# VectorE's order at the stage borders: norm-weight products and low parts of the second token tile taken by halves around the last weight split

## The reference

```
for each of the four layers:
    h = rms_norm(x, w_mix)             # x * rsqrt(mean(x^2) + eps) * w
    x = x + mixer(h)                   # gated delta rule; latent attention; differential
                                       # attention; sliding-window attention with sinks
    x = x + (silu(g) * u) @ w_down     # g, u = halves of rms_norm(x, w_ffn) @ w_gate_up
between the two blocks:  x = rms_norm(x, final_norm)
```

## Time and profile before

| | us |
|---|---|
| median of 3 runs (lowest to highest) | 1441.63 (1440.91 to 1443.24) |
| the profiled execution, its own time | 1442.56 |
| its span, first to last instruction | 1440.8 |
| TensorE busy | 1410.2 |
| VectorE busy | 927.9 |
| ScalarE busy | 728.2 |

### The profile page before, as it was taken

One profiled execution on the slowest core, in us unless ns is written; L12 is line 12 of the kernel. 1 busy time (PEld: TensorE's weight loads), 2 busy tenths in 40 slices (PEclk: granted clock), 3 DMA queues, 4 the chain that ended last, 5 costly groups with the idle time before them and its releaser, 6 DMA issues.

```text
span 1440.8 us, 19866 instructions
## 1 busy us (share of the span) xinstructions
PE 1410.2 (98%) x7787; PEld 1202.1 (83%) x7787; DVE 927.9 (64%) x1630; ACT 728.2 (51%) x1246; POOL 22.9 (2%) x44
## 2 busy tenths in 40 slices
PE   8899999999999999999999999899999999999999
PEld 8899999888888888888888878688888877888887
DVE  7767777756755547666555499775555587665553
ACT  7564646434544436545444465745444456454442
POOL 3200000000000000000000000000000000000000
PEclk9999999999999999999999999999999997999999
DMA  8433323225665554436665445246655541465552
GB/s 236 125 103 88 88 87 91 74 74 161 190 188 182 185 176 153 155 102 198 184 189 190 161 162 181 68 125 205 187 186 188 167 140 51 126 204 178 188 190 88
DMA packets 168838, 216.61 MB, mean 150 GB/s; under 512 B 11219, under 2 KB 136746, under 8 KB 168746
## 3 DMA queue, kind: packets, MB, share of 16 engines
q1 hardware_dynamic: 166976, 213.03, 47.7%
q10 hardware_dynamic: 1770, 2.32, 0.6%
HBM read 214.26 MB, written 1.05 MB: 149 GB/s over the span
## 4 chain that ended last, share of the span: by engine, by line
PE 83%; DVE 11%; DMA 2%; ACT 2%; issue 1%; POOL 1%; SPq 0%; ACTq 0%; DVEq 0%
PE psum L898 22%; PE psum L900 22%; PE psum L899 22%; PE psum L1112 4%; DVE w_low L646 4%; PE psum L1104 2%; PE psum L1296 2%; PE psum L1272 2%; PE psum L1118 1%; PE psum L1233 1%; DVE hT L2110 1%; PE psum L1285 1%; DVE work L818 1%; PE psum L1086 1%; DVE x L2088 1%
## 5 line engine op out<-in xcount | busy, mean ns | idle before, releaser
L646 DVE TENSOR_TENSOR w_low<-ring,w_high 128x1024 fp32r<-128x1024 f32 (+3 forms) x395 | 475.0, 1212 | 320.3 <-ACT w_high L632 318.2
L632 ACT ACTIVATE w_high<-ring 128x1024 fp32r<-128x1024 f32 (+3 forms) x395 | 411.1, 1048 | 441.1 <-PE psum L900 430.7
L898 PE MATMUL psum<-w_high,hT 128*128 128x512 f32 (+2 forms) x944 | 372.3, 394 | 1.5 <-DVE hT L2110 1.0
L900 PE MATMUL psum<-w_high,hT 128*128 128x512 f32 (+2 forms) x944 | 366.1, 388 | 0.0
L899 PE MATMUL psum<-w_low,hT 128*128 128x512 f32 (+2 forms) x944 | 365.5, 387 | 0.0
L898 PEld LDWEIGHTS psum<-w_high,hT 128*128 128x128 f32 x944 | 177.3, 188 | 37.3 <-DVE hT L2110 3.8
L898 PE MATMUL psum<-w_high,parts 128*128 128x512 f32 (+1 forms) x532 | 208.1, 391 | 0.3 <-DVE work L2673 0.3
L900 PEld LDWEIGHTS psum<-w_high,hT 128*128 128x128 f32 x944 | 177.2, 188 | 36.6
L900 PE MATMUL psum<-w_high,parts 128*128 128x512 f32 (+1 forms) x532 | 206.0, 387 | 0.0
L899 PE MATMUL psum<-w_low,parts 128*128 128x512 f32 (+1 forms) x532 | 205.8, 387 | 0.0
L899 PEld LDWEIGHTS psum<-w_low,hT 128*128 128x128 f32 x944 | 177.5, 188 | 33.8
(11 more groups left out here) (278 smaller groups left out, 1418.2 us busy)
## 6 DMA issues: line engine op xcount, KB each, us to landing
ring<-in_ffn_w_gate_up SPq DMA_DIRECT2D x176, 256.0 KB, 3.2
ring<-in_w_gate_up SPq DMA_DIRECT2D x176, 256.0 KB, 3.2
ring<-in_gdn_w_in SPq DMA_DIRECT2D x48, 512.0 KB, 3.9
ring<-in_ffn_w_down SPq DMA_DIRECT2D x44, 512.0 KB, 3.3
ring<-in_w_down SPq DMA_DIRECT2D x44, 512.0 KB, 3.3
ring<-in_da_w_qkv SPq DMA_DIRECT2D x24, 512.0 KB, 4.1
ring<-in_gdn_w_out SPq DMA_DIRECT2D x16, 512.0 KB, 3.3
ring<-in_mla_w_out SPq DMA_DIRECT2D x8, 512.0 KB, 4.3
```

The lines of the kernel that those rows point to most:

```text
L632: nc.scalar.activation(piece_slot(w_high, n), piece_slot(ring, n), ACT.Copy).then_inc(s.w_hi, 1)
L646: nc.vector.tensor_tensor(piece_slot(w_low, n), piece_slot(ring, n), piece_slot(w_high, n).bitcast(F32), ALU.subtract).then_inc(s.w_lo, 1)
L898: mm(out, lhs[0], rhs[0], start=start, stop=False)
L900: return mm(out, lhs[1], rhs[0], start=False, stop=stop)
```

## The change

For the six GAINED borders VectorE's order for tile 1 changes from "split, product 0, product 1, low 0, low 1" to "product 0, split, low 0, product 1, low 1". `turned_low` is cut into `gained` and `low_half`, which hold the same two instructions. At k = 5 `final_gains(0)` moves from behind turned_low of tile 0 to behind tile 1's last low part, right in front of `final_gains(1)`; ScalarE's square of the first tile's product moves with it, behind the square of x of tile 1. It gets a wait of ScalarE on itself between the two squares of the products, as both write the same scratch tile `junk_y`. k = 7 keeps its order.

```diff
--- before.py
+++ after.py
@@ -1586,9 +1586,14 @@
                 if t and k not in GAINED:
                     act.wait_ge(s.ssq_done, 2 * TURN[k] + 1)
                 last = f(junk, x[:, t, :], ACT.Square, accum_out=ssq[:, t:t + 1])
-                if k == 5:
-                    act.wait_ge(s.y_ready, t + 1)
-                    last = f(junk_y, xy[:, t, :], ACT.Square, accum_out=ssq_y[:, t:t + 1])
+                if k == 5 and t:
+                    for n in range(T):
+                        act.wait_ge(s.y_ready, n + 1)
+                        if n:
+                            own.wait()
+                        last = f(junk_y, xy[:, n, :], ACT.Square, accum_out=ssq_y[:, n:n + 1])
+                        if n == 0:
+                            own(last)
                 last.then_inc(s.ssq_done, 1)
 
             def scaled_in(k):
@@ -2099,16 +2104,23 @@
 
             def turned_low(k, t):
 
-                at = 4 * TURN[k] + 2 * t
                 for h in range(2):
                     if k in GAINED:
-                        dve.wait_ge(s.xT_psum, at + h + 1)
-                        tt(quads(xg[:, t, h, :]), quads(B[4 + 2 * t + h][:, :]), gain_row(k, h), ALU.mult).then_inc(s.xg_ready, 1)
+                        gained(k, t, h)
                 for h in range(2):
-                    dve.wait_ge(s.h_hi, at + h + 1)
-                    turned_x = xg[:, t, h, :] if k in GAINED else B[4 + 2 * t + h][:, :]
-                    tt(turned_tiles(hT, 1, t, h), quads(turned_x), turned_tiles(hT, 0, t, h).bitcast(F32),
-                       ALU.subtract).then_inc(s.h_lo, 1)
+                    low_half(k, t, h)
+
+            def gained(k, t, h):
+
+                dve.wait_ge(s.xT_psum, 4 * TURN[k] + 2 * t + h + 1)
+                tt(quads(xg[:, t, h, :]), quads(B[4 + 2 * t + h][:, :]), gain_row(k, h), ALU.mult).then_inc(s.xg_ready, 1)
+
+            def low_half(k, t, h):
+
+                dve.wait_ge(s.h_hi, 4 * TURN[k] + 2 * t + h + 1)
+                turned_x = xg[:, t, h, :] if k in GAINED else B[4 + 2 * t + h][:, :]
+                tt(turned_tiles(hT, 1, t, h), quads(turned_x), turned_tiles(hT, 0, t, h).bitcast(F32),
+                   ALU.subtract).then_inc(s.h_lo, 1)
 
             def root_of(y, w):
 
@@ -2163,15 +2175,21 @@
                     return
                 residual(pr, 0, s.x_ready)
                 turned_low(k, 0)
-                if k == 5:
-                    final_gains(0)
                 split_low(dve, end - 4 + SPLIT)
                 split_low(dve, end - 3 + SPLIT)
                 residual(pr, 1, s.x_ready)
                 split_low(dve, end - 2 + SPLIT)
-                split_low(dve, end - 1 + SPLIT)
-                turned_low(k, 1)
+                if k in GAINED:
+                    gained(k, 1, 0)
+                    split_low(dve, end - 1 + SPLIT)
+                    low_half(k, 1, 0)
+                    gained(k, 1, 1)
+                    low_half(k, 1, 1)
+                else:
+                    split_low(dve, end - 1 + SPLIT)
+                    turned_low(k, 1)
                 if k == 5:
+                    final_gains(0)
                     final_gains(1)
                 inverse_roots(k)
```

## The result

| | before | after |
|---|---|---|
| median of 11 runs, us (lowest to highest) | 1442.84 (1440.91 to 1444.12) | 1444.93 (1443.49 to 1447.14) |
| ratio after to before, 95% interval | | 1.0021 (1.0012 to 1.0029) |
| the profiled execution, us (span) | 1442.56 (1440.8) | 1444.89 (1443.1) |

The change makes the kernel slower by 0.21%; a second round of runs of the same kernel gave 1.0028 (1.0017 to 1.0040). Forecast were 1445.3 us and +3.63.

A forecast was written before the change was run, and what follows sets the result against it. TensorE was taken to set the time, except at stage borders where it waits for VectorE. Feed-forward borders 2.40 + k = 2 0.60 + k = 5 0.63 = 3.63 us on the median 1441.63 gave 1445.3; range 1442.9 to 1447.6.

The forecast's parts named there:

- What bounds the kernel: TensorE sets the time except at stage borders, where it waits for VectorE's second low half and pays any lateness in full.
- The common part, 0.60 per border: Six borders: last low part 0.60 us later each (0.45 to 0.75); 2.40 over the feed-forward borders k = 1, 3, 6, 8.
- s + 3.71: Forecast start of the last low part, from start s of the old order's last split; s + 3.12 in the old order.
- bare copy: ScalarE's copy of half 1 with nothing beside it on VectorE, between product 1 and low 1; 0.69 from product to low part.
- k = 2, 0.60: Behind k = 2 roots, split and the 6.15 us weight transfer all hang on the late square: 0.60 us again.
- The first rival: Partly absorbed: lateness behind k = 2 and k = 5 disappears in stretches waiting for transfers; 1444.0 us, chance 0.13.
- k = 5, 0.63: At k = 5 the roots start 0.63 us later, from the uncovered copy and ScalarE's hand-over to itself; range 0.5 to 1.0.
- The clock: Claim that k = 2's longer stall lowers TensorE's clock to 1.2 GHz for 10.2 us; 1447.3 us, chance 0.05.
- The second rival: The longer stall at k = 2 lowers TensorE's clock; 1447.3 us, chance 0.05.
- The faster rival: Handover pipelined by halves: new order only closes holes, 6 x 0.10, plus 0.5 at k = 5; 1440.5 us, chance 0.05.
- The profiled execution: Whole kernel: the profiled execution of 1442.56 us becomes 1446.2, by the summed 3.63.

The follow-up runs named there:

- Run 3: Against the changed kernel: new order kept at the six borders, final norm's products and squares left where they were before; 1.0029 (1.0019 to 1.0039) of before.
- run 7: Against the kernel before: last split moved behind the low parts, at k = 5 behind the second final product too; 0.9979 (0.9969 to 0.9988), 1437.96 us against 1441.06.
- Run 5: Against run 3's kernel: still by halves, but a split between each product and its low part; 1.0003 (0.9994 to 1.0011) of before.
- run 4: Against the changed kernel: old order at the borders, only the final norm's products and squares moved; 0.9998 (0.9989 to 1.0007) of before.
- run 6: Against run 3's kernel: both products, then the last split, then both low parts, final norm as before; 0.9990 (0.9982 to 0.9999) of before.

## Why the prediction was right, step by step

- **What bounds the kernel.** Right: at the four feed-forward borders the second low half ends last, and TensorE pays its lateness in full; at k = 2 and k = 5 it is VectorE's roots behind it that count. Run 3 (later by 0.60) and run 7 (earlier by 1.13) show it from both sides; run 7 also shows where it ends at the feed-forward borders, at a gain of 0.4, from where TensorE no longer waits for the low part.
- **The common part, 0.60 per border.** Right in mechanism and size: s + 3.71 forecast, 3.72 measured; 0.59 to 0.65 at the four feed-forward borders, 2.38 against 2.40. Run 5 takes the bare copy away and keeps the halves, and the loss goes with it.
- **k = 2, 0.60.** Only the size was off in the first trace (0.27), by the term that was taken as fixed, the transfer of 6.15 us. It took 5.50 that time, and the chain no longer goes through it; it took 6.31 in the second trace (0.77, 0.60 + 0.16). In run 3 it took 6.14, and the stage was 0.57 longer. A shorter transfer gives back about 0.33 and no more: the three traces in which it took 5.59 to 5.70 and the roots began as in before have -0.32 to -0.35 in this column, and 0.60 - 0.33 = 0.27. The first rival's time, 1444.0, was the nearest of the rivals, but its mechanism, lateness swallowed behind waiting for transfers, wasn't it: the transfer was issued 0.60 later, both times, and took another time.
- **k = 5, 0.63.** The roots were 0.70 later, the hand-over of ScalarE to itself being 0.09 and not 0.02. The stage was longer by 0.46 and 0.42 only, since the transfer behind it took 4.46 and 4.42 us instead of 4.71, and VectorE's wait of 0.8 fell to 0.5. So some 0.25 of the roots' 0.70 did go where the first rival had put it, by a shorter transfer and not by itself: run 3, nearly as late (0.61) and with 4.73, has the 0.63. TensorE began its second tile 0.55 earlier (0.5 forecast), and run 4 shows that this gains nothing: VectorE and not TensorE ends last there. That the moved products cost nothing is shown for the roots (0.12 later, most of it ScalarE's wait on itself, 0.09); the stage of run 4 was 0.68 and 0.39 longer, and how much of that is the move's isn't known.
- **The clock.** In both traces of the changed kernel the low stretches are those of before, 10.2 us from 1190 or 1192 and two of 3.4 behind it, and none lies at k = 2, with a stall of 1.63. The second rival is out.
- **The faster rival.** Its own condition was that VectorE has 0.69 us of other work between product 1 and low 1. Run 5 puts a split there, and some 3 us come back (run 3 stood 3.8 over before, run 5 0.5). The Trainium skill (Perfetto Trace Analysis, Optimizing Scalar/DVE Operations) says that breaking up instructions may let work end sooner where Scalar and Vector aren't saturated but cause bubbles on other engines. That didn't apply: nothing was broken up, the copies were under cover already but for 0.10, and the bubble grew from 0.50 to 1.11.
- **The profiled execution** was forecast at 1446.2 and took 1444.89, 2.33 over before instead of 3.63. Of the 1.3, 0.5 is the shorter transfers at k = 2 and k = 5, and 0.74 lies in the start, ahead of the first border that the change touches, where two traces of before differ by 1.00.
- **The difference of the medians**, 2.1, is 1.5 under the forecast; the second round has 3.65. That the time itself came out within 0.4 is in part luck: the base was 1.2 higher than the three runs behind the forecast had it, and the difference 1.5 smaller. The mechanism rests on the borders, not on this agreement.

## What to carry to other kernels

When an engine hands a half to another one and takes it back, count what lies between hand-over and take-back for the last half, not for the first: that is the time the reader sees. If independent work is to be moved over such a gap, it belongs behind the last hand-over (run 6); better still it belongs behind the whole group (run 7), if the queue itself is what ends last and the engine waits somewhere later anyway. For differences of a few tenths of a us per place, compare the same instruction's start in two traces, stage by stage, rather than the times of whole runs.

## What the runs showed of the hardware

- One and the same transfer of 512 KB, issued at the same point of the same kernel, took 5.50 or 6.31 us behind k = 2, and 4.44 or 5.18 behind k = 5, from one execution to the next. What decides it stays open: in none of these traces did another queue move anything beside it behind k = 5. At k = 2 a longer transfer lengthened the stage one for one (6.31 for 6.15: 0.77 for 0.60), and a shorter one gave back 0.33 at most.
- A wait of ScalarE on its own preceding instruction cost 0.09 us behind the reading of an accumulator (839.30 to 839.39), where a wait on VectorE's result cost 0.02 to 0.03 (646.50 to 646.52; 838.12 to 838.15).
- Stretches at the low clock (granted 0.50, 1.2 GHz) came at other places and lengths in the same kernel: a further one of 3.4 us at 933, and 23.9 us instead of 17.1 behind 1188. Together they go with 2.7 us between two executions of before.
